# The dilated projection's second weight chunk split on GpSimd, the factor spread behind three unused products, and the factor's diagonal made by four operations

## The chip, the cores and the metric

The kernel runs on one core of a Trainium2 chip. The metric is the device time of one execution in microseconds (us), lower is better. The time before is the median of three runs.

## The reference

The reference is two transformer blocks on one sequence of 512 tokens with a model width of 1024, all in float32. The first block has a mixer of two attentions, a cross attention to a memory and a SwiGLU feed-forward layer (2816 hidden units). The second has a dilated attention mixer and a convolutional feed-forward layer. The change lies at the seam between the blocks:

```python
x = x + rms_norm(swiglu(h, w_gate_up[l], w_down[l]), g_ffn_post[l])     # end of block 1
...
h = rms_norm_2(x, mixer_norm[layer])                                     # block 2
mix = dilated_attention_mixer(h, attn_w_in[j], attn_q_gain[j], attn_k_gain[j], attn_w_out[j])

def rms_norm(x, g):
    xf = x.astype(jnp.float32)
    y = xf * lax.rsqrt(jnp.mean(xf * xf, axis=-1, keepdims=True) + EPS)
    return (y * g.astype(jnp.float32)).astype(x.dtype)
```

So the sum of squares of the down projection over its 1024 features has to be known for each token before anything can be added to `x`, and `x` before the first product of `h @ w_in` of the mixer (1024 x 4608, 18 chunks of 256 columns).

## The kernel before, in words

**Products.** Every float32 operand is split in a high part (`w_hi`, `a_hi`) and the rest (`w_lo`, `a_lo`), and each product is three matmuls: high by high, low by high, high by low (L1997 to L1999, in `three`). Weights come in chunks of 128 x 2048 elements, which a table `GEMMS` lists in the order of the program. There are two slots, and chunk n lies in slot n modulo 2. A chunk is loaded by SyncE into `raw`, ScalarE (or GpSimd) copies it to `w_hi` (L823, L692), and VectorE (L1330) or GpSimd (L685) subtracts to get `w_lo`. All the functions that split take a chunk `ch` and make the one after it (`ch.next_slot`). The chunks of `dil_in`, the dilated projection, have their `w_lo` from GpSimd (`pool_splits`). `weights_split` counts finished chunks; on it wait SyncE's next load into the same slot of `raw` and, in `chunk_ready`, TensorE. `tile_done` counts finished tiles; on it waits who overwrites a slot.

**Order.** No scheduler decides anything: each engine's program is written out by hand, and each engine carries out its own in order, waiting on semaphores.

**The seam.** `ffn_down` leaves eight banks of PSUM. For each, ScalarE squares the bank (L1198) and scales a copy by the gain (L1199), and VectorE sums the squares. TensorE adds across partitions by 16 matmuls one column wide (L2289, `summed_but_last` and `summed`), ScalarE takes the root (`root_of`, L836, `tok_std`), VectorE the reciprocal (L1347, `tok_rstd`) and then the *diagonal* (L1349): the identity times the reciprocals, four blocks of 128 x 128, in a tile of 128 x 512 (its name in the rows is `work`). One float32 matmul of `ones` by the diagonal spreads the factor over all partitions (`spread`, L2327, two records each). Around it stand unused products (`stay_clocked`, L2299) whose result nobody reads: five ahead, twelve behind. `stay_clocked` waits only for the first chunk of `dil_in`, ready by then.

From the spread bank, VectorE scales and adds tiles 0 and 1 of `x` (L1459, L1461) and scales the other six (L1453), GpSimd adds these to `x` (`add_residual`, L746), ScalarE makes `a_hi` (L848) and the squares (L850), and VectorE makes `a_lo` (L1441). `opening` lets TensorE do the first chunk's products tile by tile as `a_lo` comes.

**The weights of the second chunk of `dil_in`.** ScalarE makes `w_hi` behind the root (`split_hi(Chunk(G["dil_in"], 0, 6, 0))`, L1201), and GpSimd `w_lo` in its next instruction (L752), ahead of its six adds. The slot is the one that the last chunk of `ffn_down` used; TensorE's `sem_inc(tile_done, 1)` after `down_done` frees it.

**The other uses of `invert`.** It holds the reciprocal and the diagonal, and also runs for `mem_pre` (at 341 us), `ffn_pre` (474 us) and `ffn_2` (1132 us), in which TensorE calls `spread` between two products of a chunk.

Of the kernel before, what the change touches and what calls it, by code (L numbers as in the profile page):

```python
# [27 lines left out]
CREDIT = 4  # L28
# [26 lines left out]
def plan():  # L55
    gemms, chunk, signal, freed = {}, 0, 0, {"act": 0, "dve": 0, "": 0}
    for name, n, signals, tiles, by in GEMMS:
        gemms[name] = Gemm(name, n, signals, tiles, by, chunk, signal, freed[by])
        chunk, signal, freed[by] = chunk + n, signal + n * signals, freed[by] + n * tiles
    return gemms, chunk  # L60
# [49 lines left out]
def two_blocks_kernel(nc, A, out):  # L110
    F, R = mybir.dt.float32, mybir.dt.float32r
    ALU, ACT, AX = mybir.AluOpType, mybir.ActivationFunctionType, mybir.AxisListType
    ds = bass.ds
    G, TOTAL = plan()
# [34 lines left out]
    with ctx:  # L149
        def sb(name, shape, dt=F):  # L150
            return ctx.enter_context(nc.sbuf_tensor(name, shape, dt))

        def sem(name):
            return ctx.enter_context(nc.semaphore(name))
# [11 lines left out]
        ident = sb("ident", [128, 128])  # L166
# [7 lines left out]
        tok_rstd = sb("tok_rstd", [128, 4])  # L174
# [29 lines left out]
        def region(start, *shape):  # L204
            n = 1
            for d in shape:
                n *= d
            ap = arena[:, start:start + n]
            if len(shape) == 2:
                ap = ap.rearrange("p (a b) -> p a b", b=shape[1])  # L210
            return ap

        def slots(start, n, width):

            return work[:, start:start + n * width].rearrange("p (a b) -> p a b", b=width)
# [23 lines left out]
        mem_k = region(0, KT, N_MEM)  # L239
# [26 lines left out]
        diagonal = slots(5 * S, 1, S)[:, 0, :]  # L266
# [10 lines left out]
        weights_split = sem("weights_split")  # L277
# [364 lines left out]
        def _(pool):  # L642
# [39 lines left out]
            def split_lo(ch):  # L682
                pool.wait_ge(weights_split, ch.g + (1 + CREDIT))
                pool.wait_ge(weights_hi, ch.g + 2)
                pool.tensor_tensor(w_lo[:, ch.next_slot, :], raw[:, ch.next_slot, :],  # L685
                                   w_hi[:, ch.next_slot, :].bitcast(F), ALU.subtract).then_inc(weights_split, 1)
# [45 lines left out]
            def sum_last_four(name, pre):  # L732

                pool.wait_ge(norms[pre].ready, 2 * KT)
                pool.wait_ge(norms[pre].sq, KT)
                of = x_squares[pre]
                for n in range(3):
                    pool.wait_ge(x_added[name], 2 * KT + n)
                    pool.tensor_tensor(of[:, 4, :], of[:, 4, :], of[:, 5 + n, :], ALU.add).then_inc(x_added[name], 1)

            def add_residual(name, y):

                pool.wait_ge(x_added[name], 2)
                for k in range(2, KT):
                    pool.wait_ge(norms[name].value, k + 1)
                    pool.tensor_tensor(x_t[:, k, :], x_t[:, k, :], y[:, k, :], ALU.add).then_inc(x_added[name], 1)  # L746

            pool.wait_ge(mask_ready, 3)
            for _, name, pre in OPENED.values():
                sum_squares(norms[name])  # L750
                sum_last_four(name, pre)
            split_lo(Chunk(G["dil_in"], 0, 6, 0))  # L752
            add_residual("ffn_post", y_ffn)
            for k in (4, 6):

# [59 lines left out]
        def _(act):  # L815
            def split_hi(ch):

                act.wait_ge(raw_loaded[ch.next_slot], ch.next_loads)
                if not ch.first:
                    act.wait_ge(tile_done, ch.before)  # L820
                if ch.gemm.name in ("mem_k", "dil_out") and ch.second_of_gemm:
                    act.wait_ge(weights_split, ch.g + (1 + CREDIT))
                act.activation(w_hi[:, ch.next_slot, :], raw[:, ch.next_slot, :], ACT.Copy).then_inc(weights_hi, 1)  # L823

# [8 lines left out]
            def root_of(norm, src, scale=1.0 / D):  # L833

                act.wait_ge(norm.sum, 1)
                act.activation(tok_std[:, :], src, ACT.Sqrt, bias=eps[:, :], scale=scale).then_inc(norm.std, 1)  # L836
# [6 lines left out]
            def gained_hi(name, ready, tiles=range(KT)):  # L843

                norm = norms[name]
                for k in tiles:
                    act.wait_ge(ready, k + 1)
                    act.activation(a_hi[:, k, :], x_t[:, k, :], ACT.Identity,  # L848
                                   scale=vcol(name, k)).then_inc(norm.hi, 1)
                    act.activation(x_squares[name][:, k, :], x_t[:, k, :], ACT.Square).then_inc(norm.sq, 1)  # L850
# [290 lines left out]
            for b in range(4):  # L1141
                for half in range(2):
                    n = 2 * b + half
# [49 lines left out]
            for k in range(KT):  # L1193
                norm = norms["ffn_post"]
# [3 lines left out]
                act.activation(squares[:, k % 4, :], ps[:, k, :], ACT.Square).then_inc(norm.sq, 1)  # L1198
                act.activation(y_ffn[:, k, :], ps[:, k, :], ACT.Identity, scale=vcol("ffn_post", k)).then_inc(freed_down, 1)  # L1199
            root_of(norms["ffn_post"], ps[:, 4, 0:4])  # L1200
            split_hi(Chunk(G["dil_in"], 0, 6, 0))  # L1201

            gained_hi("mixer_2", x_added["ffn_post"])
            split_hi(Chunk(G["dil_in"], 0, 6, 1))

# [113 lines left out]
        def _(dve):  # L1321
# [22 lines left out]
            def invert(norm):  # L1344

                dve.wait_ge(norm.std, 1)
                dve.reciprocal(tok_rstd[:, :], tok_std[:, :]).then_inc(norm.inverse, 1)  # L1347
                dve.wait_ge(norm.inverse, 1)
                dve.tensor_tensor(diagonal.rearrange("p (b n) -> p b n", b=4),  # L1349
                                  ident[:, :].rearrange("p (b n) -> p b n", b=1).to_broadcast([128, 4, 128]),  # L1350
                                  tok_rstd[:, :].rearrange("p (b n) -> p b n", n=1).to_broadcast([128, 4, 128]),
                                  ALU.mult).then_inc(norm.inverse, 1)

            def invert_pre(name):

# [427 lines left out]
            for b in range(4):  # L1783
                for half in range(2):
                    n = 2 * b + half
# [207 lines left out]
        def _(pe):  # L1993
# [16 lines left out]
            def chunk_ready(ch):  # L2010
                pe.wait_ge(weights_split, ch.g + 1 + CREDIT)
# [281 lines left out]
            def stay_clocked(gemm, n):  # L2293


                ch = Chunk(G[gemm], 0, 2, 0)
                chunk_ready(ch)
                for _ in range(n):
                    pe.matmul(ps[:, 6, :], w_hi[:, ch.slot, 0:128], w_hi[:, ch.slot, 0:S], start=True, stop=True,  # L2299
                              skip_group_check=True)  # L2300
# [6 lines left out]
            def summed(norm, then):  # L2307

                pe.wait_ge(norm.sq, KT)
                by_token(squares[:, 3, :], False, True).then_inc(norm.sum, 1)  # L2310
                stay_clocked(then, 5)
                spread(norm)
                stay_clocked(then, 12)

# [99 lines left out]
            for b in range(4):  # L2414
                pe.wait_ge(x_loaded[b], 16)
                for f in range(KT - 1):
                    last = x_turned(f, b)
# [6 lines left out]
            for k in range(KT):  # L2424
                pe.wait_ge(turns["xs"].read, k + 1)
                last = three(ps[0:HEADS, FORGET_BANK, :], (whi[:, k, :], wlo[:, k, :]), (a_hi[:, k, :], a_lo[:, k, :]),
                             k == 0, k == KT - 1, across=True)
                if k == KT - 1:
                    last.then_inc(tile_done, 1)
                if k == 1:  # L2430
                    pe.wait_ge(turns["x"].hi, 1)
                    for b in range(4):
                        last = x_turned(KT - 1, b)
# [4 lines left out]
            for t in range(3):  # L2438
                last = pe.transpose(ps[:, 4, t * 128:(t + 1) * 128], vec_rows[:, t, :], ident[:, :])
# [255 lines left out]
```

## Time and profile before

| | us |
|---|---|
| median of three runs (lowest, highest) | 1485.67 (1485.48, 1485.76) |
| the profiled execution, its own time | 1485.76 |
| its span, first to last instruction | 1484.0 |
| TensorE busy | 1468.0 (99%) |
| VectorE busy | 823.5 (55%) |
| ScalarE busy | 588.4 (40%) |
| GpSimd busy | 214.9 (14%) |

The span leaves out 1.8 us around the instructions. TensorE's matmuls overlap in the records and their ends are modelled, so 99% does not say that it never stood still. Over a run of 1485 us, the stretch that the change is about is some 25 us long (814 to 840 us); its rows say more than the shares. In the rows PE is TensorE, PEld its weight load, DVE VectorE, ACT ScalarE, POOL GpSimd and SPq the load queue of SyncE.

### The profile page before, as it was taken

The numbers are of one execution on the slowest core, as the hardware profiler recorded it, in microseconds if no ns is written. First come the engines' busy times: TensorE is split into PE (matmuls) and PEld (weight loads), VectorE is DVE, ScalarE is ACT, GpSimd is POOL, SyncE is SP. The second block draws the span as 40 slices with busy tenths as digits, with TensorE's granted clock in tenths as the row PEclk, the third lists the DMA queues.
The fourth block names the chain that finished last, engine by engine and source line by source line (L and its number), as shares of the span: only waits on it lengthen the run. The fifth ranks groups of instructions, "written<-read, shape, count | busy, mean of one in ns | idle before, by whom it ended". The sixth has DMA issues, their size and how long they took to land.

```text
span 1484.0 us, 21793 instructions
## 1 busy us (share of the span) xinstructions
PE 1468.0 (99%) x8300; PEld 1221.6 (82%) x8300; DVE 823.5 (55%) x1254; ACT 588.4 (40%) x913; POOL 214.9 (14%) x199
## 2 busy tenths in 40 slices
PE   9999999999999999999999999999999999999998
PEld 6888779898899888888888688888887888888887
DVE  6534664465638443344333786747766776767232
ACT  6123765552345222222324543334754433334232
POOL 0200101111021000000000755554412000000000
PEclk9999999999999999999999999999999999999999
DMA  5523104322023433333232122223113334332321
GB/s 175 199 86 110 34 2 142 114 86 86 1 86 86 113 85 101 97 87 108 89 112 87 57 86 85 85 88 105 38 29 86 85 87 111 85 113 87 112 85 57
DMA packets 152815, 132.31 MB, mean 89 GB/s; under 512 B 6300, under 2 KB 137628, under 8 KB 152740
## 3 DMA queue, kind: packets, MB, share of 16 engines
q1 hardware_dynamic: 150836, 128.11, 28.0%
q0 software_dynamic: 848, 3.17, 0.6%
q8 instruction: 50, 0.82, 0.2%
q14 instruction: 25, 0.20, 0.0%
q10 hardware_dynamic: 1056, 0.00, 0.0%
HBM read 129.15 MB, written 2.12 MB: 88 GB/s over the span
## 4 chain that ended last, share of the span: by engine, by line
PE 91%; DVE 6%; ACT 1%; POOL 1%; DMA 1%; issue 0%; SPq 0%; DVEq 0%; POOLq 0%; ACTq 0%
PE ps L1997 26%; PE ps L1999 26%; PE ps L1998 26%; PE ps L2361 3%; PE ps L2450 1%; PE ps L2468 1%; DVE rstd L1910 1%; PE ps L2547 1%; PE ps L2556 1%; PE ps L486 1%; PE ps L2371 1%; DVE w_lo L1330 1%; ACT w_hi L823 1%; DVE a_lo L1400 1%; DVE x_t L1396 1%; POOL x_t L746 1%
## 5 line engine op out<-in xcount | busy, mean ns | idle before, releaser
L1997 PE MATMUL ps<-a_hi,w_hi 128*128 128x512 f32 (+2 forms) x1784 | 666.6, 374 | 6.7 <-DVE w_lo L1330 1.7
L1999 PE MATMUL ps<-a_hi,w_lo 128*128 128x512 f32 (+2 forms) x1784 | 660.9, 370 | 0.0
L1998 PE MATMUL ps<-a_lo,w_hi 128*128 128x512 f32 (+2 forms) x1784 | 660.6, 370 | 0.0
L1997 PEld LDWEIGHTS ps<-a_hi,w_hi 128*128 128x128 f32 (+1 forms) x1784 | 335.3, 188 | 71.5 <-DVE a_lo L1441 4.1
L1999 PEld LDWEIGHTS ps<-a_hi,w_lo 128*128 128x128 f32 (+1 forms) x1784 | 335.3, 188 | 58.3
L1998 PEld LDWEIGHTS ps<-a_lo,w_hi 128*128 128x128 f32 (+1 forms) x1784 | 335.4, 188 | 57.9 <-issue 0.7
L823 ACT ACTIVATE w_hi<-raw 128x2048 fp32r<-128x2048 f32 x116 | 221.9, 1913 | 338.9 <-PE ps L1999 337.1
L1330 DVE TENSOR_TENSOR w_lo<-raw,w_hi 128x2048 fp32r<-128x2048 f32 x96 | 219.8, 2290 | 221.4 <-ACT w_hi L823 221.1
L685 POOL TENSOR_TENSOR w_lo<-raw,w_hi 128x2048 fp32r<-128x2048 f32 x22 | 101.4, 4609 | 417.2 <-ACT w_hi L823 389.5
L1832 DVE TENSOR_TENSOR arena<-ps,rstd 128x512 f32<-128x512 f32 x88 | 60.1, 689 | 161.4 <-PE ps L1999 156.3
L1910 DVE RECIPROCAL rstd<-std 128x512 f32<-128x512 f32 x24 | 80.5, 3353 | 26.3 <-ACT std L1228 26.3
L1305 ACT ACTIVATE arena<-arena,vec 128x512 f32<-128x512 f32 x44 | 35.5, 816 | 109.3 <-DVE arena L1832 109.3
L1997 PE MATMUL ps<-w_hi,a_hi 128*128 128x512 f32 x192 | 75.6, 394 | 0.4 <-DVE arena L1923 0.4
L1999 PE MATMUL ps<-w_hi,a_lo 128*128 128x512 f32 x192 | 74.9, 390 | 0.0
L1998 PE MATMUL ps<-w_lo,a_hi 128*128 128x512 f32 x192 | 74.9, 390 | 0.0
L1170 ACT ACTIVATE arena<-arena 128x512 f32<-128x512 f32 x22 | 13.9, 632 | 89.5 <-DVE arena L1832 89.5
L1975 DVE SCALAR_TENSOR_TENSOR arena<-arena,vec 128x384 f32<-128x384 f32 x88 | 47.9, 545 | 0.0
L2361 PEld LDWEIGHTS ps<-arena,work 128*64 128x64 f32 x1120 | 36.1, 137 | 13.0 <-issue 10.1
L1997 PEld LDWEIGHTS ps<-w_hi,a_hi 128*128 128x128 f32 x192 | 36.0, 188 | 9.4 <-DVE arena L1923 0.8
L1972 DVE SCALAR_TENSOR_TENSOR arena<-arena,vec 128x127 f32<-128x127 f32 x88 | 36.6, 415 | 11.7 <-DVE arena L1832 5.4
L1999 PEld LDWEIGHTS ps<-w_hi,a_lo 128*128 128x128 f32 x192 | 36.0, 188 | 7.6
L1998 PEld LDWEIGHTS ps<-w_lo,a_hi 128*128 128x128 f32 x192 | 36.1, 188 | 7.3
(251 smaller groups left out, 1309.3 us busy)
## 6 DMA issues: line engine op xcount, KB each, us to landing
raw<-in_w_gate_up SPq DMA_DIRECT2D x44, 512.0 KB, 4.7
raw<-in_ffn_w_up SPq DMA_DIRECT2D x44, 512.0 KB, 4.7
raw<-in_attn_w_in SPq DMA_DIRECT2D x36, 512.0 KB, 4.5
raw<-in_w_in SPq DMA_DIRECT2D x24, 512.0 KB, 4.7
raw<-in_w_down SPq DMA_DIRECT2D x22, 512.0 KB, 4.0
raw<-in_ffn_w_down SPq DMA_DIRECT2D x22, 512.0 KB, 4.0
raw<-in_w_mem_kv SPq DMA_DIRECT2D x16, 512.0 KB, 4.3
raw<-in_w_out SPq DMA_DIRECT2D x8, 512.0 KB, 4.0
```

Of the source, the lines that this page charges most:

```text
L685: pool.tensor_tensor(w_lo[:, ch.next_slot, :], raw[:, ch.next_slot, :], w_hi[:, ch.next_slot, :].bitcast(F), ALU.subtract).then_inc(weight ...
L823: act.activation(w_hi[:, ch.next_slot, :], raw[:, ch.next_slot, :], ACT.Copy).then_inc(weights_hi, 1)
L1305: act.activation(conv[:, 2 * ch.slot_o + j, :], up[:, 2 * ch.slot_o + j, :], ACT.Identity, bias=vcol("conv_b", ch.c + j * FT), scale=vcol( ...
L1330: dve.tensor_tensor(w_lo[:, ch.next_slot, :], raw[:, ch.next_slot, :], w_hi[:, ch.next_slot, :].bitcast(F), ALU.subtract).then_inc(weights ...
L1832: dve.tensor_tensor(up[:, 2 * ch.slot_o + j, :], ps[:, bank, :], rstd[:, :], ALU.mult).then_inc(signal, 1)
L1910: dve.reciprocal(rstd[:, :], std[:, :]).then_inc(dil_rstd, 1)
L1972: dve.scalar_tensor_tensor(out=residues(u)[:, 0:tap, 1:128], in0=residues(src)[:, 4 - tap:4, 0:127], scalar=scalar, in1=residues(u)[:, 0:t ...
L1975: dve.scalar_tensor_tensor(out=u[:, tap * 128:S], in0=src[:, 0:S - tap * 128], scalar=scalar, in1=u[:, tap * 128:S], op0=ALU.mult, op1=ALU ...
L1997: pe.matmul(dst, s_hi, m_hi, start=start, stop=False, skip_group_check=across)
L1998: pe.matmul(dst, s_hi, m_lo, start=False, stop=False, skip_group_check=across)
L1999: return pe.matmul(dst, s_lo, m_hi, start=False, stop=stop, skip_group_check=across)
L2361: last = pe.matmul(dst[c, :], stationary[:, c], moving, start=start, stop=stop, skip_group_check=True)
```

## The change

Four edits:

- GpSimd makes both parts of the second chunk of `dil_in` with `both_halves`, which waits for the load and for the slot, copies and subtracts. ScalarE's copy is gone from behind the root.
- The wait on `weights_split` in ScalarE's `split_hi` now stands for `dil_in` too, at its second chunk.
- Three unused products stand ahead of the spread, in place of five.
- `invert` makes the diagonal by four `tensor_scalar` of 128 x 128 in place of one `tensor_tensor` of 128 x 512 with both inputs broadcast. This holds in all four uses.

```diff
--- before.py
+++ after.py
@@ -749,7 +749,8 @@
             for _, name, pre in OPENED.values():
                 sum_squares(norms[name])
                 sum_last_four(name, pre)
-            split_lo(Chunk(G["dil_in"], 0, 6, 0))
+            pool.wait_ge(weights_split, Chunk(G["dil_in"], 0, 6, 0).g + (1 + CREDIT))
+            both_halves(Chunk(G["dil_in"], 0, 6, 0))
             add_residual("ffn_post", y_ffn)
             for k in (4, 6):
 
@@ -818,7 +819,7 @@
                 act.wait_ge(raw_loaded[ch.next_slot], ch.next_loads)
                 if not ch.first:
                     act.wait_ge(tile_done, ch.before)
-                if ch.gemm.name in ("mem_k", "dil_out") and ch.second_of_gemm:
+                if ch.gemm.name in ("mem_k", "dil_out", "dil_in") and ch.second_of_gemm:
                     act.wait_ge(weights_split, ch.g + (1 + CREDIT))
                 act.activation(w_hi[:, ch.next_slot, :], raw[:, ch.next_slot, :], ACT.Copy).then_inc(weights_hi, 1)
 
@@ -1198,10 +1199,6 @@
                 act.activation(squares[:, k % 4, :], ps[:, k, :], ACT.Square).then_inc(norm.sq, 1)
                 act.activation(y_ffn[:, k, :], ps[:, k, :], ACT.Identity, scale=vcol("ffn_post", k)).then_inc(freed_down, 1)
             root_of(norms["ffn_post"], ps[:, 4, 0:4])
-            split_hi(Chunk(G["dil_in"], 0, 6, 0))
-
-
-
             gained_hi("mixer_2", x_added["ffn_post"])
             split_hi(Chunk(G["dil_in"], 0, 6, 1))
 
@@ -1346,10 +1343,10 @@
                 dve.wait_ge(norm.std, 1)
                 dve.reciprocal(tok_rstd[:, :], tok_std[:, :]).then_inc(norm.inverse, 1)
                 dve.wait_ge(norm.inverse, 1)
-                dve.tensor_tensor(diagonal.rearrange("p (b n) -> p b n", b=4),
-                                  ident[:, :].rearrange("p (b n) -> p b n", b=1).to_broadcast([128, 4, 128]),
-                                  tok_rstd[:, :].rearrange("p (b n) -> p b n", n=1).to_broadcast([128, 4, 128]),
-                                  ALU.mult).then_inc(norm.inverse, 1)
+                for b in range(4):
+                    last = dve.tensor_scalar(diagonal[:, b * 128:(b + 1) * 128], ident[:, :], tok_rstd[:, b:b + 1], None,
+                                             ALU.mult)
+                last.then_inc(norm.inverse, 1)
 
             def invert_pre(name):
 
@@ -2308,7 +2305,7 @@
 
                 pe.wait_ge(norm.sq, KT)
                 by_token(squares[:, 3, :], False, True).then_inc(norm.sum, 1)
-                stay_clocked(then, 5)
+                stay_clocked(then, 3)
                 spread(norm)
                 stay_clocked(then, 12)
```

GpSimd between its third reduction for `ffn_pre` (L739 `sum_last_four`) and the adds to `x`. Before:

```order
L739 TENSOR_TENSOR arena<-arena 128x512 [waits x_added_mem_post] x2
L685 TENSOR_TENSOR w_lo<-raw,w_hi 128x2048 [waits weights_hi,weights_split]
L746 TENSOR_TENSOR x_t<-x_t,arena 128x512 [waits ffn_post_value,x_added_ffn_post]
L746 TENSOR_TENSOR x_t<-x_t,arena 128x512 [waits ffn_post_value] x5
L757 TENSOR_TENSOR arena<-arena 128x512 [waits mixer_2_sq] x2
```

Now (L758 is the old L757):

```order
L739 TENSOR_TENSOR arena<-arena 128x512 [waits x_added_mem_post] x2
L692 CAST w_hi<-raw 128x2048 [waits tile_done,raw_loaded_1,weights_split]
L685 TENSOR_TENSOR w_lo<-raw,w_hi 128x2048 [waits weights_hi,weights_split]
L746 TENSOR_TENSOR x_t<-x_t,arena 128x512 [waits ffn_post_value,x_added_ffn_post]
L746 TENSOR_TENSOR x_t<-x_t,arena 128x512 [waits ffn_post_value] x5
L758 TENSOR_TENSOR arena<-arena 128x512 [waits mixer_2_sq] x2
```

The copy comes in ahead of the subtraction and waits for the slot and the load; the subtraction no longer waits for another engine's `w_hi`.

VectorE at the seam, after the sums of squares. Before:

```order
L1341 TENSOR_TENSOR work<-work 128x512 [waits ffn_post_added,ffn_post_sq] x6
L1347 RECIPROCAL tok_rstd<-tok_std 128x4 [waits ffn_post_std]
L1349 TENSOR_TENSOR work<-ident,tok_rstd 128x512 [waits ffn_post_inverse]
L1459 TENSOR_TENSOR ps<-arena,ps 128x512 [waits freed_down,ffn_post_spread]
L1461 TENSOR_TENSOR x_t<-ps,x_t 128x512 [waits ffn_post_value]
```

Now:

```order
L1338 TENSOR_TENSOR work<-work 128x512 [waits ffn_post_added,ffn_post_sq] x6
L1344 RECIPROCAL tok_rstd<-tok_std 128x4 [waits ffn_post_std]
L1347 TENSOR_SCALAR work<-ident,tok_rstd 128x128 [waits ffn_post_inverse]
L1347 TENSOR_SCALAR work<-ident,tok_rstd 128x128 x3
L1456 TENSOR_TENSOR ps<-arena,ps 128x512 [waits freed_down,ffn_post_spread]
L1458 TENSOR_TENSOR x_t<-ps,x_t 128x512 [waits ffn_post_value]
```

One instruction became four in the same place, and only the last of the four signals TensorE.

## Rows read from the trace of the kernel before

**Rows 1.** The page: the chain that ended last, shares by engine.

```profile
PE 91%; DVE 6%; ACT 1%; POOL 1%; DMA 1%; issue 0%; SPq 0%; DVEq 0%; POOLq 0%; ACTq 0%
```

**Rows 2.** Chain of waits in order of time, 795 to 862 us (start, length, what).

```profile
820.19 0.71 DVE ps L1459
...
822.94 0.85 DVE a_lo L1441
```

**Rows 3.** Timeline of TensorE (start, length, engine, line, what, idle before), 802 to 850 us.

```profile
813.80 0.39 PE L1999 MATMUL ps<-a_hi,w_lo 128*128 128x512 f32 x1
814.50 1.92 PE L2289 MATMUL ps<-ones,work 128*128 128x1 f32 x16 [0.30 <-PE ps L1999]
816.28 2.45 PE L2299 MATMUL ps<-w_hi 128*128 128x512 f32 x5
818.52 1.62 PE L2327 MATMUL ps<-work,ones 128*128 128x512 f32 x2
819.45 3.45 PE L2299 MATMUL ps<-w_hi 128*128 128x512 f32 x12
823.89 0.47 PE L1997 MATMUL ps<-a_hi,w_hi 128*128 128x512 f32 x1 [0.99 <-POOL w_lo L685]
```

**Rows 4.** Timeline of ScalarE, 802 to 850 us.

```profile
816.45 0.26 ACT L836 ACTIVATE tok_std<-ps,eps 128x4 f32<-128x4 f32 x1 [1.05 <-PE ps L2289]
816.61 1.90 ACT L823 ACTIVATE w_hi<-raw 128x2048 fp32r<-128x2048 f32 x1
821.64 0.73 ACT L848 ACTIVATE a_hi<-x_t,vec 128x512 fp32r<-128x512 f32 x1 [3.12 <-DVE x_t L1461]
```

**Rows 5.** Timeline of VectorE, 802 to 850 us.

```profile
816.75 0.18 DVE L1347 RECIPROCAL tok_rstd<-tok_std 128x4 f32<-128x4 f32 x1 [2.55 <-ACT tok_std L836]
816.96 0.69 DVE L1349 TENSOR_TENSOR work<-ident,tok_rstd 128x512 f32<-128x512 f32 x1
...
822.85 0.93 DVE L1441 SCALAR_TENSOR_TENSOR a_lo<-x_t,vec,a_hi 128x512 fp32r<-128x512 f32 x1
```

**Rows 6.** Timeline of GpSimd, whole run.

```profile
155.03 1.89 POOL L692 CAST w_hi<-raw 128x2048 fp32r<-128x2048 f32 x1 [89.53 <-PE ps L1999]
157.07 4.56 POOL L685 TENSOR_TENSOR w_lo<-raw,w_hi 128x2048 fp32r<-128x2048 f32 x1 [0.15 <-POOL w_hi L692]
...
287.41 1.29 POOL L718 TENSOR_TENSOR work<-work 128x512 f32<-128x512 f32 x1 [3.66 <-ACT work L869]
...
818.66 4.58 POOL L685 TENSOR_TENSOR w_lo<-raw,w_hi 128x2048 fp32r<-128x2048 f32 x1 [347.49 <-ACT w_hi L823]
824.52 9.79 POOL L746 TENSOR_TENSOR x_t<-x_t,arena 128x512 f32<-128x512 f32 x6 [1.29 <-DVE arena L1453]
```

**Rows 7.** Timeline of TensorE, 152 to 157 us.

```profile
154.49 0.40 PE L1999 MATMUL ps<-w_hi,a_lo 128*128 128x512 f32 x1
```

**Rows 8.** Issue of the second chunk's load, queue of SyncE, 795 to 806 us.

```profile
796.80 0.92 SPq L599 DMA_DIRECT2D raw<-in_attn_w_in  x2
```

**Rows 9.** L1801: duration ns min/median/max, first and last start us.

```profile
L1801 DVE TENSOR_SCALAR arena<-arena,mod x4: 239/242/1239, 287.5 to 289.0; 128x32 f32<-128x32 f32 x4
```

**Rows 10.** Timeline of VectorE, 279 to 304 us: the same four.

```profile
287.52 1.71 DVE L1801 TENSOR_SCALAR arena<-arena,mod 128x32 f32<-128x32 f32 x4
```

**Rows 11.** L1787: duration ns min/median/max, first and last start us.

```profile
L1787 DVE TENSOR_SCALAR arena<-arena,row_rstd x8: 480/481/486, 254.8 to 257.6; 128x512 f32<-128x512 f32 x8
```

**Rows 12.** Tiles of a_lo on VectorE with GpSimd idle, 1118 to 1142 us.

```profile
1117.46 2.14 DVE L1441 SCALAR_TENSOR_TENSOR a_lo<-x_t,vec,a_hi 128x512 fp32r<-128x512 f32 x3
```

**Rows 13.** By stretch: us, busy time of each engine, PEclk, DMA share, GB/s.

```profile
816.20:816.40 0.20, 0.20 (x3) 0.20 (x4) 0.00 (x0) 0.00 (x0) 0.00 (x0) 0.80 0.00 0
816.40:819.60 3.20, 3.20 (x9) 2.20 (x8) 0.87 (x2) 2.06 (x2) 0.94 (x1) 0.50 0.00 0
```

**Rows 14.** The diagonal of mem_pre on VectorE, 332 to 350 us.

```profile
341.41 0.69 DVE L1349 TENSOR_TENSOR work<-ident,tok_rstd 128x512 f32<-128x512 f32 x1
```

**Rows 15.** The spread of mem_pre on TensorE, 338 to 346 us.

```profile
342.30 1.02 PE L2327 MATMUL ps<-work,ones 128*128 128x512 f32 x2
```

## The prediction

> **What bounds the kernel now.** I began with the page. The chain that ended last is TensorE for 91% and VectorE for 6% [rows 1], so the whole run tells nothing about an edit of a few microseconds: a stretch in which TensorE waits has to be found. The chain of waits for 795 to 862 us leads through the seam between the blocks. Behind the spread it goes over VectorE (820.19, and `a_lo` at 822.94) [rows 2], and TensorE's timeline shows the hole: the last product of `ffn_down` ends at 813.80 + 0.39 = 814.19, and the first of `dil_in` starts at 823.89 [rows 3]. In between it does only 16 column sums, the unused products and the spread. What ends this stretch is the factor: sums until 816.4, root at 816.45 [rows 4], reciprocal 816.75, diagonal 816.96 to 817.65 [rows 5], spread 818.52 [rows 3]. The diagonal is ready 0.87 us before the spread starts. That is the five unused products, 2.24 us from 816.28 to 818.52, or 0.45 us each. TensorE's row puts its 0.99 us of idle time before 823.89 down to GpSimd's `w_lo`. It wasn't: that `w_lo` was over at 818.66 + 4.58 = 823.24 [rows 6], and `a_lo` ended at 822.85 + 0.93 = 823.78, 0.11 us ahead of the product [rows 3, 5]. So the second chunk's weights are early enough as they are, and making them sooner gains nothing directly.
>
> **ScalarE's copy goes away.** It took 1.90 us at 816.61 [rows 4], behind the root, and ScalarE's next work comes with `x` at 821.64. Its removal is worth nothing: the wait for `x` covers it. The added wait on `weights_split` stands in front of the copy that follows the first chunk's products, long after the split it waits for: nothing.
>
> **GpSimd's new place.** Its load was issued at 796.80 [rows 8], long before. The slot is free when the last product is done, 814.19. From a product's end (154.49 + 0.40 = 154.89) to GpSimd's copy at 155.03 it took 0.14 us in the one like case [rows 6, 7]; TensorE has a wait and a signal of its own in between here and goes on at 814.50 [rows 3], so the copy starts between 814.33 and 814.64. I take 814.45. The copy takes 1.89 and the subtraction follows 0.15 later [rows 6]: 816.49, and with 4.58 us it ends at 821.07. SyncE's next load starts 2.2 us sooner and nobody waits for it.
>
> **The diagonal, the term that decides.** It is issued at 816.96 as before, now 0.47 us after GpSimd's subtraction began. What happens to a `tensor_scalar` with a column of scalars, from SBUF to SBUF, while GpSimd subtracts or adds, the trace has once. Of the four at L1801 (128 x 32) three took 0.24 us and the first 1.239 [rows 9]. It was issued at 287.52 [rows 10], while GpSimd's addition ran from 287.41 to 288.70 [rows 6], and ended at 288.76, 0.06 us after that. `a_lo`, with two tensors in SBUF, shows the same: 0.93 us, ended 0.54 after GpSimd's subtraction [rows 5, 6], against 2.14 / 3 = 0.71 with GpSimd idle [rows 12]. The Trainium skill (SBUF — State Buffer, section Who interferes with whom) says that such a Vector instruction and a GpSimd instruction exclude each other for the whole of the one that starts first. By that rule the wait is 4.1 us here, as in my sum; the rows alone show waits up to 1.2 us. So I let the first of the four wait for 821.07.
>
> Behind it: the four of L1801 ended at 287.52 + 1.71 = 289.23 [rows 10], the last three 0.157 us apart. At 512 elements the distance is 2.8 / 7 = 0.40 us [rows 11], so 128 elements cost 0.205. The first ends 0.06 + 0.05 after GpSimd, and three more make 0.73 in all: the diagonal is done at 821.80, where the single one was at 817.65. TensorE starts 0.11 us later (as at 823.89), at 821.91 and not at 818.52: **+3.39 us**. The three unused products are over at 816.28 + 3 x 0.45 = 817.6 and save nothing, since the diagonal is late. TensorE then stands still for 4.3 us.
>
> **The spread itself** took 1.62 us [rows 3], in a stretch in which the granted clock was 0.50, so 1.2 of 2.4 GHz, from about 816.3 on [rows 13]; the engine had fallen to it after two microseconds of sums one column wide. At full clock the same pair takes 1.02 [rows 15]. It will start after a stretch with less work than before, so I take the low clock for all of it, between 1.62 and twice 1.02: 1.85, **+0.23 us**. The twelve unused products then end later, but `a_lo` comes 3.7 us behind the spread and covers them, at 0.45 us each or nearly.
>
> **Relief.** GpSimd is done at 821.1, before `a_lo` of tile 0 comes: 0.93 becomes 0.71, **-0.22 us**.
>
> **The three other diagonals.** In `mem_pre` the single one runs from 341.41 to 342.10 [rows 14] and TensorE comes to the spread at 342.30 [rows 15]. Four take 3 x 0.205 + 0.29 = 0.90, until 342.31, and with 0.11 to start the spread is at 342.42: 0.12 us late. `ffn_pre` has the same pattern. **+0.25 us** for both. `ffn_2`'s has 1.5 us to spare and costs nothing. The Trainium skill (VectorE: DVE Perf Modes, section The TRN2 errata) prices a Vector instruction between SBUF tensors at 58 cycles and the elements over the speed-up: an estimate of 127 ns for each of 128 elements at double rate, 0.51 us for four, less than the single one's 0.69. By that these 0.25 us would not arise and the seam would be 0.22 us shorter, +3.2 us in all; no row has instructions of this size that close, and my sum stays with the rows.
>
> **Sum:** 3.39 + 0.23 - 0.22 + 0.25 = +3.65 us. Everything behind the seam hangs on `x` and moves with it. The profiled execution's own time is 1485.76, so 1489.4; the median of the runs shown is 0.09 lower, **1489.3 us**. A measurement of this kernel can tell about 0.2%, 3.0 us, from no change: 1488.6 is the border.
>
> **Rival 1: VectorE isn't held.** If `tensor_scalar` on the identity doesn't share what L1801 shared, or if GpSimd's subtraction starts after 816.96, the diagonal is done at 816.96 + 0.90 = 817.86 and the spread starts at 817.97: -0.55, +0.13 for more of it at low clock, -0.22, +0.25, so -0.4 us, 1485.3. It decides at 0.47 us of delay of GpSimd; L1801 speaks against it, the rounding of the slot's time for it. The Trainium skill's page on SBUF, same section, exempts a Vector instruction with one SBUF input outside the two-port modes; L1787's 481 ns for 512 elements is less than `tensor_tensor`'s 0.69, so two elements at a time.
>
> **Rival 2: the clock is back before the spread.** All of it at 2.4 GHz, 1.02 us: 0.83 less than forecast, +2.8, 1488.5. For it: 0.50 ended soon after 819.6 before [rows 13]. Against: TensorE was at work all that time, and now stands still from 817.6.
>
> **Rival 3: the clock stays low into the products of the first chunk.** Six products of a tile at 0.45 are 2.7 us, against GpSimd's pace of 9.79 / 6 = 1.63 per tile [rows 6]: about +1 us for each tile that it lasts, +1.5 over the forecast, 1490.8.
>
> **Chances.** Forecast 0.58, rival 1 0.13, rival 2 0.24, rival 3 0.05. The forecast's own range is 1488.8 to 1490.1 (the copy's start, 0.12 less or 0.19 more, the spread 1.62 to 2.04, the page's price of the four, 0.2 for what shifts). Leaving out rival 1 and the top of rival 3, the range is 1487.9 to 1490.7. Slower by over 0.2%: the forecast, a third of rival 2, rival 3: 0.70. Faster by over 0.2% has no mechanism: 0.01. The rest, 0.29, is within.
>
> **What would show it.** GpSimd's copy at 814.3 to 814.6; the first of the four diagonals some 4 us long, ended just after GpSimd's `w_lo`, the others under 0.3; the spread at 821.9 with TensorE idle ahead of it; the clock of that stretch; `a_lo` of tile 0 at 0.7. Wrong would be a diagonal done by 818, or a seam that is longer for another reason than this wait.

## The result and the profile after

The changed kernel takes **1489.78 us**, the median of ten runs (1489.29 to 1489.97), against 1485.61 (1485.44 to 1485.76) for the kernel before: a ratio of 1.0027, 95% interval 1.0019 to 1.0035, so 4.2 us slower. The forecast was 1489.3. Three executions in the batches below were far slower (4974.03 us in e3, 2088.57 and 3865.40 of the kernel before beside e11); the ratios leave them out, and the medians shown move by at most 0.02 us with them. The span of the profiled execution went from 1484.0 to 1488.0.

The timelines of the changed kernel, 813 to 832 us (start, length, engine, line, what, idle before and its releaser), of TensorE, VectorE, GpSimd and ScalarE:

```profile
814.00 0.39 PE L1996 MATMUL ps<-a_hi,w_lo 128*128 128x512 f32 x1
814.69 1.92 PE L2286 MATMUL ps<-ones,work 128*128 128x1 f32 x16 [0.30 <-PE ps L1996]
816.47 1.10 PE L2296 MATMUL ps<-w_hi 128*128 128x512 f32 x3
821.91 2.08 PE L2324 MATMUL ps<-work,ones 128*128 128x512 f32 x2 [4.34 <-DVE work L1347]
822.99 5.37 PE L2296 MATMUL ps<-w_hi 128*128 128x512 f32 x12
828.20 0.39 PE L1994 MATMUL ps<-a_hi,w_hi 128*128 128x512 f32 x1
...
816.94 0.18 DVE L1344 RECIPROCAL tok_rstd<-tok_std 128x4 f32<-128x4 f32 x1 [2.55 <-ACT tok_std L837]
817.15 4.70 DVE L1347 TENSOR_SCALAR work<-ident,tok_rstd 128x128 f32<-128x128 f32 x4
824.02 0.70 DVE L1456 TENSOR_TENSOR ps<-arena,ps 128x512 f32<-128x512 f32 x1 [2.17 <-PE ps L2324]
...
826.69 0.74 DVE L1438 SCALAR_TENSOR_TENSOR a_lo<-x_t,vec,a_hi 128x512 fp32r<-128x512 f32 x1
...
814.64 1.89 POOL L692 CAST w_hi<-raw 128x2048 fp32r<-128x2048 f32 x1 [343.44 <-PEq L2277]
816.68 4.51 POOL L685 TENSOR_TENSOR w_lo<-raw,w_hi 128x2048 fp32r<-128x2048 f32 x1
828.17 4.70 POOL L746 TENSOR_TENSOR x_t<-x_t,arena 128x512 f32<-128x512 f32 x3 [6.98 <-DVE arena L1450]
...
816.64 0.26 ACT L837 ACTIVATE tok_std<-ps,eps 128x4 f32<-128x4 f32 x1 [1.04 <-PE ps L2286]
825.47 0.72 ACT L849 ACTIVATE a_hi<-x_t,vec 128x512 fp32r<-128x512 f32 x1 [8.56 <-DVE x_t L1458]
```

The reader is to see one thing first: the four small operations at L1347 take 4.70 us, where the single one took 0.69 [rows 5], and TensorE stands still for 4.34 us until they are done. GpSimd's subtraction began 0.47 us before them and was over at 816.68 + 4.51 = 821.19. L1347 by itself, of the stretch 817 to 817.5 (only the first of the four starts there) and of the whole run (duration min/median/max in ns):

```profile
L1347 DVE TENSOR_SCALAR work<-ident,tok_rstd x1: 4110/4110/4110, 817.2 to 817.2; 128x128 f32<-128x128 f32 x1
...
L1347 DVE TENSOR_SCALAR work<-ident,tok_rstd x16: 273/281/4110, 341.3 to 1137.0; 128x128 f32<-128x128 f32 x16
```

The first takes 4.110 us, from 817.15 to 821.26, which is 0.07 us after the subtraction; the other fifteen of the run take 0.28. The chain of waits for 812 to 832 us has the same stretch (start, length, what). "issue" is time in which the engine waited for nothing that the profile shows: this hold appears in it under no semaphore.

```profile
817.19 3.99 issue
821.19 0.68 DVE work L1347 x3
```

The clock, by stretch (us; busy time of PE, PEld, DVE, ACT, POOL with counts; PEclk; DMA share; GB/s):

```profile
816.40:819.60 3.20, 1.17 (x5) 0.53 (x5) 2.62 (x2) 0.26 (x1) 3.05 (x2) 0.61 0.00 0
819.60:821.90 2.30, 0.00 (x0) 0.00 (x0) 2.25 (x4) 0.00 (x0) 1.58 (x1) 0.50 0.00 0
...
824.00:827.00 3.00, 3.00 (x8) 2.32 (x8) 2.91 (x5) 1.44 (x3) 0.00 (x0) 0.50 0.56 192
827.00:828.20 1.20, 1.20 (x5) 0.93 (x5) 1.20 (x3) 1.05 (x2) 0.03 (x1) 0.86 0.00 0
```

The granted clock is at 1.2 GHz from about 817.1 to 827.3, where before it was back at full speed soon after 819.6 [rows 13].

### The profile page after: what moved, and what is told of

Read it like the earlier page. It is cut to its first block, busy times and chain, and to the rows that moved or that the text cites. A ratio compares the mean times of both kernels' runs of the same rounds, so it can differ in the third digit from the quotient of the medians.

```text
span 1488.0 us, 21801 instructions
## 1 busy us (share of the span) xinstructions
PE 1469.1 (99%) x8298; PEld 1222.2 (82%) x8298; DVE 827.7 (56%) x1266; ACT 586.6 (39%) x912; POOL 216.8 (15%) x200
## 3 DMA queue, kind: packets, MB, share of 16 engines
HBM read 129.15 MB, written 2.12 MB: 88 GB/s over the span
## 4 chain that ended last, share of the span: by engine, by line
PE 90%; DVE 6%; ACT 1%; POOL 1%; issue 1%; DMA 1%; SPq 0%; DVEq 0%; POOLq 0%; ACTq 0%
PE ps L1994 26%; PE ps L1995 26%; PE ps L1996 26%; PE ps L2358 3%; PE ps L2447 1%; PE ps L2465 1%; DVE rstd L1907 1%; PE ps L2544 1%; PE ps L2553 1%; PE ps L486 1%; PE ps L2368 1%; DVE w_lo L1327 1%; POOL x_t L746 1%; ACT w_hi L824 1%; DVE a_lo L1397 1%
## 5 line engine op out<-in xcount | busy, mean ns | idle before, releaser
L692 POOL CAST w_hi<-raw 128x2048 fp32r<-128x2048 f32 x3 | 5.7, 1891 | 441.7 <-PEq L2277 343.4
```

## One yardstick for all kernels

Two executions reach the seam some tenths of a microsecond apart, so starts are not compared, only distances. Three of them add up to the seam: from the end of the last product of `ffn_down` to the start of the spread (**A**), from there to VectorE's first operation on `x`, L1459 before and L1456 after (**B**, the length of the spread), and from there to GpSimd's first add to `x` (**C**, in which `a_lo` of tile 0 lies). Before: 814.19 to 818.52, to 820.19 and to 824.52 [rows 2, 3, 6], so 4.33, 1.67 and 4.33. After: 814.39, 821.91, 824.02, 828.17.

A, B and C are those of the one profiled execution of each kernel, the medians those of nine to eleven executions.

| kernel | A | B | C | seam | median, us | kernel before, same batch |
|---|---|---|---|---|---|---|
| before | 4.33 | 1.67 | 4.33 | 10.33 | 1485.61 | |
| the change | 7.52 | 2.11 | 4.15 | 13.78 | 1489.78 | 1485.61 |
| e1, one operation | 7.39 | 2.11 | 4.16 | 13.66 | 1488.95 | 1485.67 |
| e2, weights as before | 3.69 | 2.11 | 4.53 | 10.33 | 1486.20 | 1485.67 |
| e3, before with three unused | 3.52 | 2.11 | 4.72 | 10.35 | 1485.77 | 1485.67 |
| e4, twelve ahead | 7.57 | 2.06 | 4.16 | 13.79 | 1489.06 | 1485.71 |
| e5, halves, four operations | 7.46 | 2.12 | 4.15 | 13.73 | 1489.67 | 1485.71 |
| e6, halves, one operation | 5.25 | 2.11 | 4.15 | 11.51 | 1486.86 | 1485.71 |
| e7, subtraction behind | 3.69 | 2.11 | 4.16 | 9.96 | 1485.70 | 1485.71 |
| e8, diagonal on ScalarE | 4.09 | 1.86 | 4.15 | 10.10 | 1486.03 | 1485.67 |
| e9, e7 with one operation | 3.51 | 1.67 | 4.21 | 9.39 | 1485.03 | 1485.72 |
| e10, e9 with five unused | 3.51 | 2.09 | 4.15 | 9.75 | 1485.12 | 1485.72 |
| e11, e9 with ten operations | 4.47 | 2.11 | 4.15 | 10.73 | 1486.42 | 1485.78 |

The change's seam is 3.45 us longer: A +3.19, B +0.44, C -0.18. The rest of the 4.0 us lies elsewhere, and the marks of GpSimd (it does the same work in both kernels) say where: two of its additions, at 334.25 and 467.11 before, stand 132.86 us apart there and 133.03 after, so `mem_pre` costs 0.17; from there to the end of `ffn_down` it is +0.15 for `ffn_pre`; and 0.3 more come in near 1070 us, of which more below.

## The experiments

The theory was that VectorE is held by GpSimd's subtraction for as long as that lasts. The rivals were that the four operations are slow, that the low clock of TensorE does it, or that the earlier copy shifts something else. Numbers of lines differ between the kernels with the edit.

**e1, one operation.** The change, with the diagonal made by the old `tensor_tensor`.

```diff
-                for b in range(4):
-                    last = dve.tensor_scalar(diagonal[:, b * 128:(b + 1) * 128], ident[:, :], tok_rstd[:, b:b + 1], None,
...
+                dve.tensor_tensor(diagonal.rearrange("p (b n) -> p b n", b=4),
```

> The change, but with the diagonal by one tensor_tensor of 128x512 as before, in all four uses. Theory (GpSimd's subtraction holds VectorE): it is held just as the four were, until GpSimd's w_lo ends at about 821.1; being one operation it ends some 0.1 us sooner behind that, and mem_pre and ffn_pre get back 0.15 us each: 1489.3, 0.4 to 0.5 under the change. Rival (it is the four operations that are slow beside GpSimd, one is not held): the diagonal is done at 817.9 and the time is 1485.2.

Measured 1488.95 (ratio 1.0021, 1.0012 to 1.0031). Timeline of VectorE and GpSimd at the seam:

```profile
816.87 4.58 DVE L1346 TENSOR_TENSOR work<-ident,tok_rstd 128x512 f32<-128x512 f32 x1
...
816.39 4.51 POOL L685 TENSOR_TENSOR w_lo<-raw,w_hi 128x2048 fp32r<-128x2048 f32 x1
```

The single one is held as well: 4.58 us, where it takes 0.69 alone. The four operations are not the cause of the seam's length. Of the 0.83 us by which the median is lower, 0.74 are accounted for: 0.12 of the seam, 0.32 of `mem_pre` and `ffn_pre`, and 0.3 near 1070 us, which this kernel doesn't have (e11). The expectation, 1489.3, lacked this last term and was 0.35 too high.

**e2, weights as before.** The change without its first two edits: only the three unused products and the four operations are left.

```diff
-            pool.wait_ge(weights_split, Chunk(G["dil_in"], 0, 6, 0).g + (1 + CREDIT))
-            both_halves(Chunk(G["dil_in"], 0, 6, 0))
+            split_lo(Chunk(G["dil_in"], 0, 6, 0))
...
             root_of(norms["ffn_post"], ps[:, 4, 0:4])
+            split_hi(Chunk(G["dil_in"], 0, 6, 0))
```

> The change, with ScalarE's w_hi behind the root and GpSimd's w_lo after it, as before; three unused products and the four operations stay. Theory: nothing of GpSimd's runs beside the diagonal (its w_lo starts at 818.7), the diagonal is done 0.9 us after it was issued, the spread starts 3.7 us after the last product of ffn_down against 4.3 before, and the time is 1485.5 (1485.2 to 1485.8). Rival (the clock: with three unused products TensorE has too little to do and loses its clock for 10 us): at least 1487.

Measured 1486.20 (1486.02 to 1486.47; ratio 1.0003, 0.9994 to 1.0012). The loss is gone, so it came with GpSimd's new place. But the time is 0.7 us above the 1485.5 expected. Timeline of VectorE and GpSimd:

```profile
817.13 0.87 DVE L1347 TENSOR_SCALAR work<-ident,tok_rstd 128x128 f32<-128x128 f32 x4
...
822.84 1.12 DVE L1438 SCALAR_TENSOR_TENSOR a_lo<-x_t,vec,a_hi 128x512 fp32r<-128x512 f32 x1
...
818.83 4.58 POOL L685 TENSOR_TENSOR w_lo<-raw,w_hi 128x2048 fp32r<-128x2048 f32 x1 [347.66 <-ACT w_hi L823]
```

The spread comes 0.64 us sooner (A), but takes 0.44 more at the low clock (B), and the earlier `a_lo` runs into GpSimd's subtraction, which lasts until 823.41: 1.12 us, 0.20 more (C). Nothing is left of the gain at the seam (10.33 us, as before), and what is over it in the median, 0.53 us, is about what the other diagonals and the place near 1070 us add (0.32 + 0.3).

**e3, before with three unused.** The kernel before, with `stay_clocked(then, 3)` in place of 5 ahead of the spread.

```diff
-                stay_clocked(then, 5)
+                stay_clocked(then, 3)
```

> The kernel before with three unused products ahead of the spread and nothing else. Theory: the spread starts 0.11 us behind the diagonal, 0.75 us sooner than before, less some 0.1 for more of it at the low clock: 1485.0. Rival (the clock): low for longer, no gain or up to 1 us slower.

Measured 1485.77 (ratio 1.0001, 0.9991 to 1.0010): a miss of the gain expected, by the same exchange as in e2: A -0.81, B +0.44, C +0.39. Timeline of VectorE:

```profile
822.27 1.31 DVE L1441 SCALAR_TENSOR_TENSOR a_lo<-x_t,vec,a_hi 128x512 fp32r<-128x512 f32 x1
```

GpSimd's subtraction ends at 818.43 + 4.59 = 823.02 here, and `a_lo` 0.56 after it, as before. In this order the end of `a_lo` hangs on GpSimd and not on the spread.

**e4, twelve ahead.** The change, with `stay_clocked(then, 12)` ahead of the spread, to part the wait from the clock.

```diff
-                stay_clocked(then, 3)
+                stay_clocked(then, 12)
```

> The change with twelve unused products ahead of the spread in place of three, so that TensorE works on until about 821.3 while it waits for the diagonal. Theory: the diagonal is done at 821.8 as in the change, the spread starts within 0.1 us of the change's, but at 2.4 GHz, in 1.0 to 1.1 us and not 2.08: 1488.8, 1 us under the change. That is all that the clock costs. Rival (the low clock is what makes the change slow, the wait is only part): under 1487.

Measured 1489.06 (ratio 1.0022, 1.0013 to 1.0032). Timeline of TensorE:

```profile
816.39 2.99 PE L2296 MATMUL ps<-w_hi 128*128 128x512 f32 x12
821.88 2.02 PE L2324 MATMUL ps<-work,ones 128*128 128x512 f32 x2 [2.50 <-DVE work L1347]
```

And by stretch, the wait for the diagonal and the spread:

```profile
819.40:821.80 2.40, 0.00 (x0) 0.00 (x0) 2.40 (x4) 0.00 (x0) 1.76 (x1) 1.00 0.00 0
822.00:825.00 3.00, 3.00 (x6) 1.67 (x7) 1.02 (x2) 0.00 (x0) 0.00 (x0) 0.50 0.90 300
```

Twelve in 2.99 us, 0.25 each: here they ran at the full clock, and the low clock lasted 3.41 us in all (821.98 to 825.39), as in the kernel before, against 10.24 in the change. The seam is as long as the change's all the same (13.79 and 13.78). So the long stretch of low clock isn't the cause; what the clock adds to the path over the kernel before is the 0.4 us of the spread.

The expectation missed in two ways. TensorE did not work on until 821.3: at the full clock the twelve were over at 819.38. And the spread took 2.02 us, not 1.0 to 1.1: the granted clock was full while TensorE stood still and fell at about 822.0, some 0.1 us after the spread had begun. Why it fell there was not settled. The profiled execution, 1489.52, is one of the four slower ones of ten (1489.52 to 1489.74); the other six took 1488.62 to 1489.07, about what was expected with a spread at the full clock, but no trace shows one of them.

**e5 and e6, the subtraction in halves.** GpSimd subtracts 128 x 1024 twice; e5 with the four operations, e6 with one.

```diff
+                n = CHUNK // parts
+                for a in range(parts):
+                    last = pool.tensor_tensor(w_lo[:, ch.next_slot, a * n:(a + 1) * n], raw[:, ch.next_slot, a * n:(a + 1) * n],
+                                              w_hi[:, ch.next_slot, a * n:(a + 1) * n].bitcast(F), ALU.subtract)
...
-            both_halves(Chunk(G["dil_in"], 0, 6, 0))
+            both_in_parts(Chunk(G["dil_in"], 0, 6, 0), 2)
```

> The change with GpSimd's subtraction of 128x2048 cut in two of 128x1024, with no wait between them; the diagonal stays four operations. Theory: VectorE's first operation gets in when the first half ends (about 819.0); then GpSimd's second half gets in between the first and the second of the four and holds the others until about 821.5. Spread as late as in the change or up to 0.3 us later: 1489.8 to 1490.1. Rival (once in, VectorE's four go through together): spread at 819.8, 1487.6.

> The same two halves with the diagonal by one operation of 128x512. Theory: it waits for the first half alone, ends about 0.6 us after it (819.6), the spread starts 2.2 us sooner than in the change: 1487.0 (1486.8 to 1487.6). Rival (the hold is not per instruction): like e1.

Measured 1489.67 and 1486.86; the first is 0.13 us under its range, with A 0.06 shorter than in the change and not longer, the second within its range. The diagonal of e6, timeline of VectorE and GpSimd:

```profile
816.94 2.42 DVE L1359 TENSOR_TENSOR work<-ident,tok_rstd 128x512 f32<-128x512 f32 x1
...
816.46 5.10 POOL L704 TENSOR_TENSOR w_lo<-raw,w_hi 128x1024 fp32r<-128x1024 f32 x2
```

And of e5, the one line of the diagonal by stretch, 817 to 817.5 and 819.2 to 821.2, and the two halves on GpSimd:

```profile
L1360 DVE TENSOR_SCALAR work<-ident,tok_rstd x1: 1959/1959/1959, 817.1 to 817.1; 128x128 f32<-128x128 f32 x1
...
L1360 DVE TENSOR_SCALAR work<-ident,tok_rstd x1: 2376/2376/2376, 819.0 to 819.0; 128x128 f32<-128x128 f32 x1
...
L704 POOL TENSOR_TENSOR w_lo<-raw,w_hi x2: 2338/2346/2355, 816.7 to 819.0; 128x1024 fp32r<-128x1024 f32 x2
```

This is the sharpest pair. With one operation the hold is halved, and GpSimd's second half waits for VectorE in its turn: it took 2.789 us against 2.355 for the first half (5.10 for both, 4.65 in e5). With four, the first is through at 817.14 + 1.96 = 819.10, the second half starts meanwhile, and the second operation, issued at 819.02, is held for 2.376 us: the three behind the first gain nothing from the halves. In both kernels the hold goes by instructions: whoever started first was let through to its end, and then the other.

**e7, the subtraction behind the diagonal.** GpSimd copies early, then waits for the diagonal (`norms["ffn_post"].inverse`, 2) and subtracts.

```diff
+                pool.tensor_copy(w_hi[:, ch.next_slot, :], raw[:, ch.next_slot, :]).then_inc(weights_hi, 1)
+                pool.wait_ge(norms["ffn_post"].inverse, 2)
+                split_lo(ch)
...
-            both_halves(Chunk(G["dil_in"], 0, 6, 0))
+            low_behind_diagonal(Chunk(G["dil_in"], 0, 6, 0))
```

> The change, but GpSimd waits for the finished diagonal between its copy and its subtraction (norm.inverse at 2). Theory: the copy ends before the diagonal is issued, nothing is held, the spread starts 3.7 us after the last product; GpSimd's subtraction then runs from 818.1 to 822.7 and may hold a_lo of tile 0 for 0.2 us: 1485.5 (1485.2 to 1485.9). Rival (the move of the copy from ScalarE to GpSimd costs by itself): over 1487.

Measured 1485.70 (ratio 1.0000, 0.9990 to 1.0009). Timeline of VectorE and GpSimd:

```profile
817.33 0.88 DVE L1355 TENSOR_SCALAR work<-ident,tok_rstd 128x128 f32<-128x128 f32 x4
...
818.29 4.56 POOL L685 TENSOR_TENSOR w_lo<-raw,w_hi 128x2048 fp32r<-128x2048 f32 x1 [1.58 <-DVE work L1355]
```

All four edits of the change are in it, the early copy too; only the overlap isn't. It costs 1.6 us of GpSimd's time and gives back the whole loss. The seam is even 0.37 us shorter than before, which the other diagonals and the place near 1070 us take back. Whether GpSimd's copy would hold VectorE too, no run shows: in all of them it is over before the reciprocal.

**e8, the diagonal on ScalarE.** The change, with the four blocks of `ffn_post` made by ScalarE behind the reciprocal, while GpSimd subtracts; VectorE leaves `invert` of this norm behind the reciprocal.

```diff
+            act.wait_ge(norms["ffn_post"].inverse, 1)
+            for b in range(4):
+                last = act.activation(diagonal[:, b * 128:(b + 1) * 128], ident[:, :], ACT.Identity,
+                                      scale=tok_rstd[:, b:b + 1])
+            last.then_inc(norms["ffn_post"].inverse, 1)
```

> The change, with the diagonal of this one norm made by ScalarE (four activations of 128x128 with the reciprocal as scale) while GpSimd's copy and subtraction stay where the change has them. Theory (what holds VectorE is shared by VectorE and GpSimd alone): ScalarE isn't held, its four end about 1 us after the reciprocal, the spread starts 4 us after the last product, and the time is 1485.6 (1485.2 to 1486.2) with GpSimd as busy as in the change. Rival (GpSimd's long instruction slows anything that reads the identity or SBUF, or the clock is what costs): over 1487.5.

Measured 1486.03 (ratio 1.0002, 0.9992 to 1.0011). Timeline of ScalarE and GpSimd:

```profile
817.11 1.28 ACT L1204 ACTIVATE work<-ident,tok_rstd 128x128 f32<-128x128 f32 x4 [0.25 <-DVE tok_rstd L1349]
...
816.63 4.53 POOL L685 TENSOR_TENSOR w_lo<-raw,w_hi 128x2048 fp32r<-128x2048 f32 x1
```

ScalarE isn't held: same tiles, same moment, 0.3 us each, with GpSimd's subtraction running until 821.16. What is held here is VectorE by GpSimd.

**e9 and e10, only the edits that pay by the rows.** e9 is e7 with the old single operation in all four uses; e10 has five unused products again.

```diff
+                pool.wait_ge(norms["ffn_post"].inverse, 2)
...
+                dve.tensor_tensor(diagonal.rearrange("p (b n) -> p b n", b=4),
```

> The kernel e7 with the diagonal made by one tensor_tensor again: GpSimd copies early, subtracts behind the diagonal, three unused products. If the accounting by rows holds, the two diagonals of mem_pre and ffn_pre give back 0.3 us and the one of the seam 0.2: 1485.2 to 1485.5, with the spread of the seam at 818.0 to 818.1 and GpSimd's subtraction at 818.1. If four operations cost no more than one where nobody holds them, it is e7's 1485.7.

> The kernel e9 with five unused products ahead of the spread, as before the change. The spread starts at 818.5, when the fifth unused product is done, 0.4 us later than in e9, which costs 0.2 to 0.4 us if its length is the same: 1485.5 to 1485.9. If the longer work ahead brings the full clock back sooner, the spread takes 1.6 us or less in place of 2.1 and the time is that of e9 or less, 1485.0 to 1485.4.

Measured 1485.03 (1484.49 to 1485.46) and 1485.12 (1484.43 to 1485.60) against 1485.72 for the kernel before beside them: both have the ratio 0.9995, interval 0.9986 to 1.0004. The medians are 0.7 and 0.6 us lower, which the interval doesn't tell from no change; the profiled seams are 0.94 and 0.58 us shorter. Timelines of TensorE, e9 and then e10:

```profile
817.69 1.64 PE L2332 MATMUL ps<-work,ones 128*128 128x512 f32 x2 [0.49 <-DVE work L1354]
```

```profile
816.25 1.41 PE L2304 MATMUL ps<-w_hi 128*128 128x512 f32 x5
817.68 2.06 PE L2332 MATMUL ps<-work,ones 128*128 128x512 f32 x2
```

The median of e9 is 0.17 us below the range expected. Its seam began 0.39 us sooner than e7's, so the spread came at 817.69 and not at 818.0; it was 1.64 us long, where e7's was 2.07, since in this trace the clock fell only at about 818.2, in the middle of it. The expectation for e10 was wrong. I had the five unused products at 0.45 us each, and they took 0.28, because the clock fell later than in the kernel before. They hold nothing back then; in the kernel before the same five held the spread for 0.87 us. Of the 0.94 us of e9, 0.82 is in A.

**e11, nine more instructions.** A stall far from the seam was left: near 1070 us, one instruction of the dilated attention. Timeline of VectorE in the kernel before and in the change, where it comes 4.0 us later with all that was added ahead of it:

```profile
1067.55 0.42 DVE L1541 CUSTOM_DVE_ANT_0 work<-ps,masks 128x256 f32<-128x256 f32 x1 [1.05 <-PE ps L2547]
...
1071.58 0.43 DVE L1538 CUSTOM_DVE_ANT_0 work<-ps,masks 128x256 f32<-128x256 f32 x1 [1.40 <-PE ps L2544]
```

The same instruction waits 1.39 or 1.40 us in the change and in e2, e4, e5 and e7, which have nine more instructions on VectorE ahead of it (three in each of three uses of `invert`). It waits 1.04 or 1.05 in the kernel before, e1, e3, e6, e8, e9 and e10, which have none more, or five (e8). e11 is e9 with nine more in one place, the diagonal of `ffn_post` in ten operations.

```diff
+                if norm is norms["ffn_post"]:
+                    for b, at, n in [(0, 32 * q, 32) for q in range(4)] + [(1, 32 * q, 32) for q in range(4)] + [
+                            (2, 0, 128), (3, 0, 128)]:
+                        last = dve.tensor_scalar(diagonal[:, b * 128 + at:b * 128 + at + n], ident[:, at:at + n],
+                                                 tok_rstd[:, b:b + 1], None, ALU.mult)
```

> In all five kernels with four operations in every diagonal, one VectorE instruction of the dilated attention near 1070 us starts 0.35 us later behind its input than in the five kernels with one operation; those five kernels have nine more VectorE instructions ahead of it. This is the kernel e9 (one operation in mem_pre and ffn_pre) with the diagonal of ffn_post alone cut into ten operations (eight of 128 x 32, two of 128 x 128), so again nine more, all in one place. If the number of instructions ahead of it makes the delay, the idle time at that instruction is 1.40 us and the stretch from GpSimd's copy at 1042 us to its last subtraction but one is 76.8 us, not 76.5. If what is done in mem_pre and ffn_pre makes it, it is 1.04 and 76.5. The seam itself is longer by what ten operations take over one, at 0.15 to 0.2 us each about 1.0 to 1.5 us, so 1486.0 to 1486.9.

Measured 1486.42 (1486.12 to 1486.62; ratio 1.0003, 0.9993 to 1.0013), inside what was expected, the ten operations taking 1.65 us. Timeline of VectorE near 1068 us:

```profile
1068.40 0.42 DVE L1553 CUSTOM_DVE_ANT_0 work<-ps,masks 128x256 f32<-128x256 f32 x1 [1.39 <-PE ps L2559]
```

The stall is back with nothing changed in `mem_pre` and `ffn_pre`. From GpSimd's copy near 1043 us to its last subtraction but one are 77.06 us here, as in the change (77.08); in e9 it is 76.46. That is 0.60 more, not the 0.3 expected, because at this mark a second 0.3 us has come in, near 1117 us; e8 has it too, without the first (76.81). It is made up by the last subtraction, where 84.84 stands against 84.53 in e9 and 84.57 in e8. So the stall near 1070 us hangs on how many instructions VectorE has ahead of it. What it waits for there the trace doesn't say, and I leave it open; what makes the second 0.3 us wasn't tested.

## Why the prediction was right

**The hold** was the term that decided, and it held by its own steps. The copy began 0.25 us after the last product's end (forecast 0.26), the subtraction 0.15 after the copy's end. The first of the four was held until 0.07 us after the subtraction (forecast 0.06). That A is +3.19 and not +3.39 has three small reasons: the subtraction took 4.51, not 4.58; from its end to that of the fourth operation it was 0.66, not 0.73; TensorE started 0.06 after that, not 0.11. That the spread starts at 821.91, to the hundredth where the forecast had it, is luck: the stretch ahead was 0.20 us late, and the sum held that apart. The Trainium skill (SBUF — State Buffer, section Who interferes with whom) says that such a VectorE instruction and one of GpSimd exclude each other for the whole of the one that starts first. The runs agree, with 4.11 us in the change, 2.42 and 2.376 with halves, and none when the diagonal came first (e7) or from ScalarE (e8). Before the change only one row, of 1.239 us [rows 9], had shown a `tensor_scalar` held like this, and a wait of four microseconds was longer than any row had shown.

**The spread** was mis-sized: B grew by 0.44 and not by 0.23. I took 1.85 us, between 1.62 and twice 1.02, and it was 2.08, the upper end: all of it at 1.2 GHz (0.50 in the rows above). In the sum this error of +0.21 cancels the -0.20 of the hold, which is luck too. The 1.62 of before had a part at the full clock.

**The relief of `a_lo`** was forecast as -0.22; it was 0.74 us in place of 0.93, -0.19.

**The other diagonals** were mis-sized by little: 0.17 and 0.15, 0.32 in place of 0.25. Four operations take 0.87 us there, where the forecast had 0.90. By the 58 cycles of the Trainium skill (VectorE: DVE Perf Modes, section The TRN2 errata) the four would take 0.51 us, an estimate, and the same section says that this figure comes out short for single instructions. The trace shows 0.28 us for each and 0.87 together, so the price of 0.51 doesn't hold here, and the cost that it would have left out was there.

**The rivals.** Rival 1, VectorE not held, is refuted by the 4.110 us row. Rival 2, the clock back before the spread, by B. Rival 3, low clock into the first chunk's products, nearly came: the clock was low until about 827.3, and the twelve unused products took 5.37 us, not 3.45, so the first product started 0.77 us after `a_lo` was ready at 827.43. The forecast had said that `a_lo`, 3.7 us behind the spread, covers the twelve at 0.45 us each. It doesn't, and by these numbers of its own it couldn't: twelve take 5.4. This step of the prediction was wrong, but it cost nothing, since from there on GpSimd's adds, begun at 828.17, set the pace, and TensorE waits for the next `a_lo` again.

**Not in the sum** were the 0.3 us near 1070 us. The sum of 3.65 has 3.45 + 0.32 against it, and with 0.3 about the profiled execution's 4.0. The median moved by 4.17, inside the forecast's own range of 1488.8 to 1490.1.

## What to carry to other kernels

Before work is moved to an earlier place on GpSimd, look at what VectorE has to do while it runs: here a long instruction between SBUF tensors on the one held a short one on the other until it was done, and the loss is that of the short one's place in the chain, not of its size. Put the long one behind the short one, by a wait if need be (e7), or give the short one to ScalarE (e8). Cutting the long one helps only if VectorE asks once: with several short instructions in a row the next piece got in behind the first of them, and they were held twice (e5). And a gain just ahead of a shared wait is worth only what the wait's other end leaves (e2, e3).

## What the hardware showed that I had not expected

- The moment at which the clock falls behind the 16 one-column sums differs between traces whose TensorE program is the same up to there. Five unused products took 2.24 us in the kernel before [rows 3] and 1.41 in e10; twelve took 2.99 in e4. The spread was 1.62 to 2.08 us long with it.
- In the change the clock stayed at 1.2 GHz for 10.24 us, in e6 for 6.83 and in e4 and the kernel before for 3.41. TensorE stood still for 4.34, 2.22, 2.50 and 0 us ahead of the spread in these. The idle time alone doesn't order them: e5 has 4.45 us of it and e11 0.82, and both had the low clock for 6.8 us.
- One VectorE instruction starts 0.35 us later behind its input when nine more instructions stand ahead of it in VectorE's program, in both placements tried (three in each of three places, or nine in one), and not with five more (e11, e8). The cause is open.
